# The Hyena projection of the context: pairs of tiles by seven quarter products instead of eight slices a tile

## The reference

```python
def hyena_mixer(h, w_in, b_in, short_w, short_b, w1, b1, w2, b2, w3, freq, filt_bias, w_out, b_out):
    L = h.shape[1]
    u = centred_depthwise_conv(h @ w_in + b_in, short_w, short_b)
    v, x1, x2 = jnp.split(u, 3, axis=-1)
    filt = hyena_filters(L, w1, b1, w2, b2, w3, freq)
    z = x1 * two_sided_fft_conv(v, filt[:, 0, 0], filt[:, 0, 1], filt_bias[0])
    z = x2 * two_sided_fft_conv(z, filt[:, 1, 0], filt[:, 1, 1], filt_bias[1])
    return z @ w_out + b_out
```

## Time and profile before

| | us |
|---|---|
| median of three runs | 3102.27 (3101.62 to 3105.03) |
| the profiled execution | 3100.76 |
| its span in the profile | 3098.6 |
| TensorE busy in the span | 2978.1 |
| VectorE, ScalarE, GpSimd busy | 1505.4, 724.1, 390.4 |
| the stage of the change | about 1427 to 1523 us of the span |

### The profile page before, as it was taken

How to read it: one execution, slowest core, us unless ns; L and a number is a source line. 1 busy time by engine, 2 the same in 40 slices (tenths; PEclk the granted TensorE clock), 3 DMA queues, 4 the chain that set the end, 5 groups by cost and what they waited for, 6 DMA issues and landing times.

```text
span 3098.6 us, 36760 instructions
## 1 busy us (share of the span) xinstructions
PE 2978.1 (96%) x14781; PEld 1672.5 (54%) x14781; DVE 1505.4 (49%) x2837; ACT 724.1 (23%) x1524; POOL 390.4 (13%) x274
## 2 busy tenths in 40 slices
PE   8999899999989999999999999999999988999998
PEld 5888544788844444557657433333346545444443
DVE  5994862898394255886666211211155743111212
ACT  1211541131163211121124100110025642111111
POOL 3544000555300010020001000000000000000000
PEclk9999999999999999999999999999999999999999
DMA  5452002357200312202313999999921005999997
GB/s 227 154 215 84 28 1 109 147 190 275 81 12 14 134 58 85 108 34 70 143 55 128 409 382 391 390 380 374 388 81 66 1 3 206 421 421 420 421 421 294
DMA packets 89895, 605.86 MB, mean 196 GB/s; under 512 B 10806, under 2 KB 11607, under 8 KB 19328
## 3 DMA queue, kind: packets, MB, share of 16 engines
q1 hardware_dynamic: 79776, 575.70, 46.5%
q0 software_dynamic: 4432, 15.73, 1.7%
q10 hardware_dynamic: 5520, 12.09, 1.2%
HBM read 592.47 MB, written 11.01 MB: 195 GB/s over the span
## 4 chain that ended last, share of the span: by engine, by line
PE 62%; DVE 8%; ACT 2%; issue 1%; DVEq 0%; ACTq 0%
PE ps L2966 7%; PE ps L2928 7%; PE ps L1605 5%; PE ps L2979 4%; PE ps L2945 4%; PE ps L3009 4%; PE ps L1122 3%; PE ps L1406 3%; PE ps L3259 2%; PE ps L2816 2%; PE ps L3018 2%; PE ps L2833 2%; PE ps L1895 2%; PE ps L2730 2%; PE ps L3422 1%; PE ps L1520 1%
## 5 line engine op out<-in xcount | busy, mean ns | idle before, releaser
L637 PE MATMUL ps<-mem 128*128 128x256 f32 x1792 | 394.9, 382 | 10.3 <-DVE mem L667 9.4
L637 PEld LDWEIGHTS ps<-mem 128*128 128x128 f32 x1792 | 341.6, 191 | 62.8 <-DVE mem L667 12.9
L582 POOL TENSOR_TENSOR mem<-mem 128x512 f32<-128x512 f32 (+1 forms) x160 | 300.0, 1875 | 530.7 <-DVE mem L878 272.4
L780 DVE SCALAR_TENSOR_TENSOR mem<-mem 128x1024 f32<-128x1024 f32 x160 | 255.5, 1637 | 13.5 <-DMA mem<-in_ada_w 12.8
L2966 PE MATMUL ps<-mem 128*64 128x512 f32 x1024 | 223.3, 594 | 0.0
L2928 PE MATMUL ps<-mem 128*64 128x512 f32 x1024 | 222.5, 592 | 0.7 <-ACT mem L2862 0.7
L667 DVE TENSOR_TENSOR mem<-ps,mem 128x256 f32<-128x256 f32 x308 | 121.4, 419 | 111.9 <-PE ps L637 68.5
L1122 PE MATMUL ps<-mem 128*128 128x512 f32 x384 | 169.6, 597 | 1.8 <-DVEq L169 1.8
L1605 PE MATMUL ps<-mem 128*128 128x512 f32 x384 | 167.0, 594 | 0.2 <-ACT mem L1235 0.2
L3118 DVE TENSOR_TENSOR mem<-ps,mem 128x512 f32<-128x512 f32 x16 | 11.1, 692 | 313.7 <-PE ps L2928 313.7
L2966 PEld LDWEIGHTS ps<-mem 128*64 128x64 f32 x1024 | 72.1, 137 | 150.6 <-issue 150.6
(11 more groups left out here) (440 smaller groups left out, 4399.0 us busy)
## 6 DMA issues: line engine op xcount, KB each, us to landing
mem<-in_moe_w SPq DMA_DIRECT2D x384, 1024.0 KB, 14.1
mem<-in_w_in SPq DMA_DIRECT2D x48, 1024.0 KB, 7.3
mem<-in_ada_w SPq DMA_DIRECT2D x48, 1024.0 KB, 5.0
...
```

Source lines behind the costliest of these rows:

```text
L582: gp(out, x, y, op).then_inc(A.mark(sem), 1)
L637: m = mm(seven(l, unit), x[:, k, :], y[:, k, :], start=(k == 0), stop=(k == 3))
L780: stt(PRODUCT if again else w, w, 1.0, C_ROWS[:, z, :], ALU.mult, ALU.mult, accum_out=mod(layer, b // KD, b % KD, z))\
```

## The change

The projection of the context is rearranged. Two tiles (256 output channels) and the 256 tokens are taken as a 2x2 arrangement of 128x128 results, and the 1024 input channels as two halves of four slices. Each pair of tiles b then takes seven products (Strassen's scheme in Winograd's form), each of four accumulating matmuls of 128x128 with 128 columns, where there were sixteen matmuls with 256 columns for the two tiles.

- GpSimd (`pool_hy_ctx`) forms four sums of weight quarters per pair, 128x512 each and in a chain, into six buffers; it waits for the landed weights itself and for the product that last read the buffer.
- VectorE (`right_sums`) forms four sums of input quarters once, after the last slice of the input; R0 and R1 are chained. Five small operations (`biases`) prepare a bias for the middle tap, since the projection's bias is no longer added at eviction: the two edge columns hold its negative instead of zero.
- TensorE (`pe_hy_ctx`) writes product 7b + i to bank (7b + i) mod 6 and waits before it for the read of the product six before. Banks 6 and 7 hold the filter network's results. The first filter's four matmuls come in two pairs: after product (8, 6) and after product (9, 4), the second pair waiting for VectorE's reads of the first (`filter_used`).
- ScalarE (`act_hy_ctx`) copies the first product of each pair and applies the middle taps of the pair before, after `j_ready`. The two sines stand between its first copies, the loads of the filter's weights behind the second sine and after pair 4's copy.
- VectorE (`joined`) adds the other six products in seven operations, with the outer taps of the pair before between the fourth and the fifth; in pair 9 two filter multiplications stand there too, and the other two with the eight folds follow it.

`quarter(s, t, i, k)` (L563) is the weight block of tile t + i and half k. The diff, cut to its core (names of the callers change from `_a` to `_ctx`; `dve_filter_layer` and `dve_filter_turned` hold the operations of the former `dve_filter_layers`, and the latent stage calls them in the old order but for the wait for the first sine):

```diff
-        def dve_filter(A, y, n, j, done, bank, biased=None):
+        def dve_filter(A, y, n, j, done, bank, biased=None, ms=range(4)):
 
             w = window_slot(A.e, y, n, j)
-            for m in range(4):
+            for m in ms:
                 A.e.wait_ge(S["filter_full"], done + m + 1)
                 tt(y.HE[:, m, j, :], ps[:, bank + m, :], w[:, m, :], ALU.mult).then_inc(A.mark("filter_used"), 1)
-            if j == 0:
+            if j == 0 and 0 in ms:
                 A.e.wait_ge(*A.last)
                 tt(y.HE[0:1, 0, 0, :], y.HE[0:1, 0, 0, :], FB, ALU.add).then_inc(A.mark(biased), 1)
 
...
+        CTX_TILES = [v(KS_ + 2064 + i * (TC + 2), TC + 2) for i in range(4)]
+        CTX_LEFT = [v(FOLD_ + i * 512, 4, P) for i in range(6)]
+        NO_BIAS, TAP_BIAS = v(UT_[0] + 512, 24), v(UT_[0] + 536, 24)
+        HC = v(HT_ + KD * T, KD, TC)
+        HY_PAIRS, HY_BANKS = 12, 6
+        FILTER_PAIR = {(8, 6): 0, (9, 4): 1}
+        def ctx_right(i, k):
+            return HC[:, 4 * i:4 * i + 4, P * k:P * k + P]
+        CTX_RIGHT = [v(EVEN_ + 1024, 4, P), v(EVEN_ + 1536, 4, P), ctx_right(0, 1), v(UT_[0], 4, P)]
+        def ctx_left(b, i):
+            return CTX_LEFT[(4 * b + i) % 6]
+        def ctx_product(b, i):
+            return ps[:, (7 * b + i) % HY_BANKS, 0:P]
+        def ctx_corner(b, i, k):
+            return CTX_TILES[(2 * b + i) % 4][:, 1 + P * k:1 + P + P * k]
+        def pool_hy_ctx(A):
+            gp = nc.gpsimd.tensor_tensor
+            A.last, A.counts = None, {}
+            for b in range(HY_PAIRS):
+                n = DEPTH * N_HYB + HY_SLOTS[0] + b // 2 * 2
+                for half in range(2):
+                    A.e.wait_ge(S[f"w_in{PLACE[n + half]}"], LANDED[n + half])
+                w = lambda i, k: quarter(PLACE[n], 2 * b % 4, i, k)
+                x = [ctx_left(b, i) for i in range(4)]
+                SUMS = ((w(1, 0), w(1, 1), ALU.add), (x[0], w(0, 0), ALU.subtract),
+                        (w(0, 0), w(1, 0), ALU.subtract), (w(0, 1), x[1], ALU.subtract))
+                for i, (one, two, op) in enumerate(SUMS):
+                    if 4 * b + i >= 6:
+                        b_, i_ = divmod(4 * b + i - 6, 4)
+                        A.e.wait_ge(S["product"], 7 * b_ + (2, 1, 3, 5)[i_] + 1)
+                    if A.last:
+                        A.e.wait_ge(*A.last)
+                    gp(x[i], one, two, op).then_inc(A.mark("weights"), 1)
+            A.last, A.counts = None, {}
+        def act_hy_ctx(A, y):
             e = A.e
             L = y.L
+            def sine(r):
+                A.e.wait_ge(S["b_ready"], r + 1)
+                act(v(H2_, L, p=(64, P)[r]), v(y.Q_, L, p=(64, P)[r]), ACT.Sin).then_inc(A.mark("c_ready"), 1)
+            def first_product(b):
+                A.e.wait_ge(S["product"], 7 * b + 1)
+                if b >= 2:
+                    A.e.wait_ge(S["dve_out"], 2 * (b - 1))
+                act(ctx_corner(b, 0, 0), ctx_product(b, 0), ACT.Copy).then_inc(A.mark("copied"), 1)
+            def middle_tap(b):
+                A.e.wait_ge(S["j_ready"], b + 1)
+                for j in (2 * b, 2 * b + 1):
+                    act(y.U3[:, j, :], CTX_TILES[j % 4][:, 1:L + 1], ACT.Identity, bias=TAP_BIAS[:, j:j + 1], scale=gv("hy_sw", 24 + j))\
+                        .then_inc(A.mark("k_ready"), 1)
             pairs = [(v(FWD_, 4 * y.ne * y.H), a[f"k_fwd_{y.tag}"]), (v(INV_, 4 * y.ne * (y.H + 1)), a[f"k_inv_{y.tag}"]),
                      (v(HR_, L, p=33), a[f"k_pos_{y.tag}"]), (v(FB_, 64, p=33), a["hy_ffn_w1_2"]),
                      (v(FB_ + 64, P, p=64), a["hy_ffn_w2_2"])]
             act_mod_norm(A, y.n, v(KS_, KD, L), v(y.Q_, L), 0, 0, 1, loads=pairs)
...
+            first_product(0)
+            sine(0)
+            first_product(1)
+            sine(1)
+            A.e.wait_ge(S["e_ready"], 2)
+            load_filter_out(e, S["const_in"], 0)
+            middle_tap(0)
+            for b in range(2, HY_PAIRS):
+                first_product(b)
+                middle_tap(b - 1)
+                if b == 4:
                     e.wait_ge(S["const_in"], 16 * 8)
                     load_filter_out(e, S["const_in"], 1, 1)
+            middle_tap(HY_PAIRS - 1)
             A.e.wait_ge(S["const_in"], 16 * 11)
             end_phase(A)
...
+        def pe_hy_ctx(A, y, st):
             L = y.L
             pe_norm(A, v(KS_, KD, L), v(y.Q_, L), L, 7, 1, y.norm_banks, (4, 9, 4))
...
+            for b in range(HY_PAIRS):
+                if b % 2 == 0:
                     s = st.get()
...
+                w = lambda i, k: quarter(s, 2 * b % 4, i, k)
+                SL, R = [ctx_left(b, i) for i in range(4)], CTX_RIGHT
+                PRODUCTS = ((w(0, 0), ctx_right(0, 0), 0, 0), (SL[1], R[1], 2, 2), (SL[0], R[0], 0, 0), (SL[2], R[2], 3, 3),
+                            (w(0, 1), ctx_right(1, 0), 0, 0), (SL[3], ctx_right(1, 1), 4, 0), (w(1, 1), R[3], 0, 4))
+                for i, (one, two, lefts, rights) in enumerate(PRODUCTS):
+                    if 7 * b + i >= HY_BANKS:
+                        b_, i_ = divmod(7 * b + i - HY_BANKS, 7)
+                        A.e.wait_ge(*((S["product_read"], 6 * b_ + i_) if i_ else (S["copied"], b_ + 1)))
+                    if lefts:
+                        A.e.wait_ge(S["weights"], 4 * b + lefts)
+                    if rights and b == 0:
+                        A.e.wait_ge(S["data_folded"], rights)
+                    for k in range(4):
+                        if b == 0 and i == 0:
+                            A.e.wait_ge(S["h_ready"], k + 1)
+                        m = mm(ctx_product(b, i), one[:, k, :], two[:, k, :], start=(k == 0), stop=(k == 3))
+                        if b and b % 2 == 0 and i == 0 and k == 0:
+                            m.then_inc(S["w_used"], 2)
+                    m.then_inc(A.mark("product"), 1)
+                    if (b, i) == (0, 3):
+                        A.e.wait_ge(S["const_in"], 16 * 5)
+                        mm(ps[0:64, 6, 0:L], v(FB_, 64, p=33), v(HR_, L, p=33), start=True, stop=True).then_inc(A.mark("e_ready"), 1)
+                    if (b, i) == (1, 2):
+                        A.e.wait_ge(S["c_ready"], 1)
+                        mm(ps[:, 7, 0:L], v(FB_ + 64, P, p=64), v(H2_, L, p=64), start=True, stop=True).then_inc(A.mark("e_ready"), 1)
+                    if (b, i) in FILTER_PAIR:
+                        pair = FILTER_PAIR[b, i]
+                        if pair == 0:
+                            A.e.wait_ge(S["const_in"], 16 * 8)
+                            A.e.wait_ge(S["i_ready"], 1)
+                        for r in range(2):
+                            if pair:
+                                A.e.wait_ge(S["filter_used"], r + 1)
+                            pe_filter(A, y, 0, 2 * pair + r, 6 + r)
+                if b == HY_PAIRS - 1:
                     st.done(A)
...
+                elif b % 2:
                     st.next()
             end_phase(A)
...
+        def dve_filter_layer(A, y, r, bank, full, reduced):
             L = y.L
...
+            A.e.wait_ge(S[full], r + 1)
+            rows = (64, P)[r]
...
+        def dve_filter_turned(A, y, sines):
+            L = y.L
+            A.e.wait_ge(S[sines], 2)
             nc.vector.memset(y.H2[:, L:L + 1], 0.0).then_inc(A.mark(), 1)
             A.e.wait_ge(*A.last)
             nc.vector.tensor_copy(y.HR, y.H2[:, ::-1]).then_inc(A.mark("i_ready"), 1)
...
             A.e.wait_ge(*A.last)
             stt(o, u[:, 2:L + 2], gv("hy_sw", 48 + j), o, ALU.mult, ALU.add).then_inc(A.mark("dve_out"), 1)
...
+        def dve_hy_ctx(A, y):
             L = y.L
+            def right_sums():
+                r00, r01, r10, r11 = ctx_right(0, 0), ctx_right(0, 1), ctx_right(1, 0), ctx_right(1, 1)
+                R = CTX_RIGHT
+                A.e.wait_ge(S["h_ready"], KD)
+                for out, one, two in ((R[0], r01, r00), (R[1], r11, R[0]), (R[2], r11, r01), (R[3], r10, R[1])):
+                    tt(out, one, two, ALU.subtract).then_inc(A.mark("data_folded"), 1)
+                    A.e.wait_ge(*A.last)
+            def biases():
+                taps = [gv("hy_sw", 24 * i, 24) for i in range(3)]
+                ts(NO_BIAS, gv("hy_b_in", 0, 24), -1.0, None, ALU.mult).then_inc(A.mark(), 1)
+                tt(TAP_BIAS, taps[0], taps[1], ALU.add).then_inc(A.mark(), 1)
+                A.e.wait_ge(*A.last)
+                tt(TAP_BIAS, TAP_BIAS, taps[2], ALU.add).then_inc(A.mark(), 1)
+                A.e.wait_ge(*A.last)
+                tt(TAP_BIAS, TAP_BIAS, gv("hy_b_in", 0, 24), ALU.mult).then_inc(A.mark(), 1)
+                A.e.wait_ge(*A.last)
+                tt(TAP_BIAS, TAP_BIAS, gv("hy_sb", 0, 24), ALU.add).then_inc(A.mark(), 1)
+                A.e.wait_ge(*A.last)
+            def outer_taps(b):
+                for j in (2 * b, 2 * b + 1):
+                    u, o = CTX_TILES[j % 4], y.U3[:, j, :]
+                    A.e.wait_ge(S["k_ready"], j + 1)
```

(40 more changed lines are left out.)

91 lines of the change are left out of this document (19 added, 72 removed).

## The result

The changed kernel takes **3127.83 us** (median of four runs, 3125.03 to 3130.94) against 3101.99 (3101.62 to 3105.03) of the kernel before, run beside it: **1.0081 times as long, interval 1.0068 to 1.0094**. Slower was the likeliest sign of the forecast, but the measured time lies above its 3111.5 us and above its upper end of 3121. The profiled execution took 3129.63 us.

The account below looks back on a forecast made before the run. TensorE bounds the stage. Matmuls -6.5, start +2.6, +0.7 and +0.5, VectorE's order +2.0, +3.6 and +1.5 gave +4.4; contention +4.8 made +9.2, hence 3110.0 profiled and 3111.5 us median; range 3101 to 3121.

Parts of the forecast that it names:

- Matmuls, -6.5: TensorE's context projection: 672 records of 128 columns at 0.114 us, 76.6 us against 83.1 for 384 of 256 columns; -6.5 us.
- rival D: TensorE's projection: the weight load paces products of 128 columns, +18.1 us more, 3125 us; chance 0.05.
- The start's wait for R1, +2.6: Stage start: product (0,1) waits for two chained VectorE subtractions after the last input slice, until 1438.15 us; +2.6 us.
- The order on VectorE: VectorE's fixed order of additions, taps and filter work reaches TensorE late in three places: +2.0, +3.6 and +1.5 us.
- pair 9: TensorE loses 2.4 us waiting for `filter_used` behind (9,4), then 0.9 before (11,0) and 0.3 at (11,3); +3.6 us.
- the tail: Stage end: last addition, ScalarE's middle tap and four outer taps take 3.45 us after the last matmul, today 2.0; +1.5 us.
- Place 1, the sine layers: Early pairs: VectorE's sine layers and ScalarE's DMA issues delay (1,0), (2,0) and (2,3) by 0.5, 0.5 and 1.0; +2.0 us.
- GpSimd beside VectorE in the stage, +4.0: GpSimd's sums slow VectorE's SBUF-only operations on the late chain; bounds from nothing to 6.5 us, +4.0 taken.
- GpSimd beside VectorE at the start, +0.8: Norm before the stage's products: five bias operations and squares slowed beside GpSimd delay ScalarE's root; 0.3 to 2.0, +0.8 taken.
- The clock: TensorE's granted clock in the stage: falling below 1.00 in the gaps would make the forecast wrong; given no price.
- Rival C: GpSimd becomes the bound: 48 sums at 2.04 + 0.04 us take 99.8 us; +13.9, 3116 us; chance 0.15.
- The range's upper end: Whole kernel: 4.4 without contention, 8.5 of full contention and 4.0 for pitch 0.120 give +17 us, rounded out to 3121.

## Why the prediction was wrong

- **Matmuls, -6.5**: right in kind, 0.115 a record and -5.8 for 0.114. Without the sums the same 368 records take 41.36 us, 0.112. Nothing of rival D. By the rule of a wider gap for a stream of load and matmul, in the Trainium skill ("TensorE: Matmul & The Clock Gate", Back-to-back issue gap), which the prediction weighed, an estimate would be 1.45 x 0.114 = 0.165. It is not borne out for these float32 records: they have 0.115, where half the pitch of 256 columns is 0.108.
- **The start's wait for R1, +2.6**: a pause of 2.72, and 2.63 without sums. Right.
- **The order on VectorE**: pair 9 right (2.19 and 0.89 measured without sums for 2.4 and 0.9), the tail right (+1.3 for +1.5). Place 1, the sine layers, was wrong as such: 0.20 without sums, for 2.0. With sums it appears, 1.56 + 2.86 + 0.20.
- **GpSimd beside VectorE in the stage, +4.0**: the pauses of the changed kernel exceed those of the run without sums by 17.73 - 9.31 = 8.4 us. Half of it was priced. The step that failed is the price by size, "0.27 for a tap of 256": a held-up operation is not slower in proportion to its columns, it lasts until the sum is over, some 0.8 to 1.1 more, whether it has 256 columns or 24. The rows that it took the price from said so already: 1.06 more at 1024 columns, 1.12 more at 512. A pair's taps in the middle of the stage cost 1.8 more, not 1.1.
- **GpSimd beside VectorE at the start, +0.8: the step that failed most.** Measured +7.0 from the first square to the spread. I named the five biases, the squares and the root, and bounded them from "0.3 to 2.0", each by itself. In truth the biases move the squares into the sums' full length (3.85 us more for four), which puts the root 4.6 us later, and TensorE's clock drops to 0.50, so that its spare matmuls take 4.21 instead of 2.27 and the spread another 2.4 later. So two things failed: the size, since squares and biases were not priced at a whole sum each, and the wait of the spread behind spare matmuls at the low clock, which no term had.
- **The clock was given no price**, and the prediction named that as what would make it wrong. The groups behind pauses took 5.6 us more in the stage, the next stage's start 2.7. In pair 9, with the pause kept and the clock held up, 3.3 of the 3.4 us came off, so there the slow groups are a cost of their own; for the other pauses no run shows it.
- **Rival C, GpSimd as the bound**, would have given 3116 us by sums of 2.04. They took 1.21. The time passed 3116 without it. **The range's upper end**, +17, had contention at its bounds, 6.5 in the stage and 2.0 at the start, and the pitch at 0.120. It was passed because the start took 7.0 and the clock, at nothing in it, 5.6 in the stage and 2.7 behind it. (Its five bounds for the stage add up to 6.6, and the input sums end at 1438.11, not 1438.15; nothing hangs on either.)

The sum of the differences on the stage: forecast +9.2, measured +24.0; 6.5 from the start, 5.6 from the clock, 0.7 from the pitch, and 1.9 from the pauses together (15.6 for 9.7 by order and 4.0 by contention; the sine layers' error and the price per operation partly cancel there) make 14.7 of the 14.8. That they add up so well is in part luck: one trace of the same code can differ from the next by 2 us.
